# Two triangular inverses moved from 64x64 to 32x32 tiles, in a two-block kernel on one core

## Chip, cores and metric

The kernel runs on one core of a Trainium2 chip, in float32 throughout. The metric is the device time of one execution in microseconds (us); the time before is the median of three runs.

## What is computed

Two blocks of a language model, sequence 512, width 1024. Block one projects its normed input and feeds two mixers, RWKV-7 (8 heads of 64) and stick-breaking attention (8 heads of 64). Block two is a gated delta rule run in both directions (16 value heads of 128, 8 key heads), then a mixture of 32 experts and an embedding gate. What matters here are two linear recurrences:

```python
# RWKV-7, per head
sa = einsum(state, -kk_t)
state = state * w_t + sa * b_t + v_t * k_t
# gated delta rule, chunked
lhs = eye + einsum(k * beta, k) * decay * (1 - eye)
u = triangular_solve(lhs, v * beta)
w = triangular_solve(lhs, k * beta * exp(gc))
```

Both are computed in chunks of 128 steps. A chunk needs T = (I - N)^-1 for a strictly triangular 128x128 matrix N (the sign is folded into N).

## The kernel before

**The inverse by doubling.** T starts as the identity. Level lv (0 to 6, `LEVELS = 7`) joins diagonal blocks of 2^lv rows into blocks of twice the size: the new off-diagonal part is T N T, restricted to that part. Level 0 copies N's own entries. Each level 1 to 6 computes V = N T^T in one set of matmuls, brings V and T to SBUF as operands, computes T V in a second set and writes the wanted entries into T^T. Up to level 5 all that is not zero lies in two 64x64 blocks on the diagonal, so the kernel keeps these alone, 64 columns side by side, and works in 64x64 tiles of TensorE, one on rows 0 to 63 and one on rows 64 to 127. Level 6 (`top`) joins the two halves off the diagonal. `quad[:, lv]` is the byte mask of the entries that a level adds; `copy_predicated` writes them.

**First loop** (L550 to L732 on TensorE, body run four times, once for each pair of RWKV heads; three in a hardware loop, the last apart). TensorE's order is: stick-breaking scores and remainders, the decay and gate products, Q and A (L621, L626), the levels (L648 to L675), the scan over four chunks (L690 to L719), then the norm's sums (L722, L726). For each of two heads h a level issues V (L659, L656 at the top) and, by a product with the identity, T turned round (`flipped`, L638); ScalarE copies both to SBUF (L825, L828); then TensorE issues T V (L674) and VectorE writes the masked part into `TTc` (L1021, after `hold`, a copy of one column at L185). Between levels stand the stick-breaking outputs (L645) and one sum of squares (L668). POOL copies the two finished diagonal blocks into `TT_` (L915) after level 5. `NEXT` lists six products of 8 matmuls that the next pair needs (L539, 128x512 each). `fill` puts 40 of these 48 matmuls into the scan, ten to a chunk by `SLOT = [0, 3, 5, 8, 10]`, behind RU (L694, L695), U (L704), S1 (L710, L711) and Y (L716 to L718); eight more stand between the sums. The stick-breaking weights for them are waited for in chunk 0. In the last pair nothing fills the scan. L572 (the stick-breaking gate product, bank 7) waits for both instructions of L952.

**Heads** (Python loop, unrolled: a first head, seven turns, a last part). A turn projects and convolves q, k, v of one key head while the scan of the head before runs between the products (L1315, L1337 to L1374); then come two z parts (L1326), and `levels` (L1422 to L1478). A head has 16 matrices (four chunks, two directions, two value heads), in two groups g of eight. N^T is formed by a product with the identity (L1430). A level runs V g0, V g1, T g0, T g1 (V: L1449, T: L1471), so that one group's copies lie beside the other's products. ScalarE copies V (L1673); VectorE writes the masked entries into `TTgc` (L1966) and turns them with `transpose`, which works on 32x32 blocks inside a row of partitions (L1971). The top level is L1445 and L1457, the last products L1471, and VectorE scales the result by beta into `TTg` (L2008, L1992). Behind level 2 stand the tokens of v (L1403), behind level 3 those of k (L1410), in level 5 the turned outputs (L1419), behind level 5 the z part 2, at the top the z part 3 (16 matmuls of the trace each, L1326). VectorE also does the attention masks (L1955), silu, and the norm of the outputs (L1930, L1935, L1949) between the levels.

Each engine runs its instructions in the order in which they are written; a `Steps` counter and a semaphore link them (`.at("V 0 3")` is the point at which V of group 0, level 3 was done). `admitted` only counts.

## Time and profile before

| | us |
|---|---|
| median of three runs | 2036.21 |
| lowest, highest | 2033.58, 2037.46 |
| the profiled execution's own time | 2028.58 |
| its span | 2026.8 |
| setup, to the first products | 81.7 |
| one pair of the first loop (first three) | 127 to 129 |
| one turn of the heads | 91.0 |

Times in the profile count from the start of the span. PE is TensorE's matmuls, PEld its weight loads, DVE VectorE, ACT ScalarE, POOL GpSimd. One float32 matmul of the code is two matmuls (and two weight loads) in the profile.

### The profile page before, as it was taken

How to read it: one execution, taken by the hardware profiler on the slowest of the kernel's cores; microseconds unless marked ns; L12 is line 12 of the kernel's file. 1: busy time of each engine (PE TensorE's matmuls, PEld its weight loads, DVE VectorE, ACT ScalarE, POOL GpSimd, SP SyncE). 2: the span in 40 equal slices, each digit the busy share in tenths (PEclk: the TensorE clock that was granted, in tenths of full speed). 3: DMA queues.
4: the chain of work that ended last, by engine and by line, in shares of the span. 5: the costliest groups of instructions: out<-in, count | busy, mean ns of one | idle time of the engine just before them, and what ended most of it. 6: DMA issues, size and time to landing. Idle time of an engine off the chain costs nothing.

```text
span 2026.8 us, 38852 instructions
## 1 busy us (share of the span) xinstructions
PE 1742.4 (86%) x16211; PEld 1135.6 (56%) x16211; DVE 907.8 (45%) x1907; ACT 631.6 (31%) x1208; POOL 127.7 (6%) x247
## 2 busy tenths in 40 slices
PE   0799999999988889999999999999699647777777
PEld 0447466574663457768686777768544523333333
DVE  5223061340621355868677686868402531111162
ACT  1133152431520153545445363545200101111112
POOL 8201000010000000000000000000000010000020
PEclk9999999999977999999999999999899669999989
DMA  8211030110821221111112111111040069999851
GB/s 321 65 43 45 0 86 2 42 45 0 305 90 52 70 66 43 43 43 44 44 42 84 44 43 43 43 43 44 15 166 11 32 253 413 407 417 397 360 176 42
DMA packets 122364, 229.15 MB, mean 113 GB/s; under 512 B 9294, under 2 KB 92587, under 8 KB 109931
## 3 DMA queue, kind: packets, MB, share of 16 engines
q1 hardware_dynamic: 100480, 194.40, 26.6%
q10 hardware_dynamic: 17996, 24.24, 3.3%
q0 software_dynamic: 3744, 8.40, 1.2%
q8 instruction: 114, 1.87, 0.4%
q14 instruction: 30, 0.25, 0.0%
HBM read 203.81 MB, written 28.44 MB: 115 GB/s over the span
## 4 chain that ended last, share of the span: by engine, by line
PE 45%; DVE 11%; DMA 10%; issue 1%; ACT 1%; SPq 0%; DVEq 0%; POOL 0%; ACTq 0%; POOLq 0%
PE ps L1315 11%; DMA W<-in_moe_w_up_dram 9%; PE ps L2209 6%; PE ps L1326 4%; PE ps L2517 4%; PE ps L1085 3%; PE ps L1471 3%; PE ps L2675 2%; PE ps L1449 2%; DVE W L1966 2%; PE ps L1354 1%; PE ps L1364 1%; PE ps L1374 1%; DVE W L1971 1%; DVE arena L1849 1%
## 5 line engine op out<-in xcount | busy, mean ns | idle before, releaser
L1315 PE MATMUL ps<-hT,W 128*128 128x512 f32 x512 | 230.2, 594 | 1.4 <-ACT hT L1109 1.0
L2517 PE MATMUL ps<-W,yT 128*32 128x256 f32 x2048 | 125.4, 400 | 45.4 <-DMA W<-in_moe_w_up_dram 33.9
L1315 PEld LDWEIGHTS ps<-hT,W 128*128 128x128 f32 x512 | 94.9, 190 | 98.2 <-issue 96.4
L539 PE MATMUL ps<-hT,W 128*128 128x512 f32 x288 | 137.9, 612 | 0.0
L2517 PEld LDWEIGHTS ps<-W,yT 128*32 128x32 f32 x2048 | 69.3, 115 | 106.7 <-DMA W<-in_moe_w_up_dram 41.1
L1326 PE MATMUL ps<-W,hT 128*128 128x256 f32 x512 | 117.3, 382 | 0.0
L2209 PE MATMUL ps<-W,yT 128*128 128x512 f32 x256 | 112.2, 601 | 0.9 <-ACT yT L1662 0.9
L1326 PEld LDWEIGHTS ps<-W,hT 128*128 128x128 f32 x512 | 94.8, 190 | 12.7
L1449 PE MATMUL ps<-W,arena 64*64 64x64 f32 x2560 | 89.9, 222 | 13.9 <-DVE W L1966 13.3
L1849 DVE SCALAR_TENSOR_TENSOR arena<-ps,arena 128x510 f32<-128x510 f32 (+1 forms) x128 | 95.6, 747 | 13.8 <-ACT arena L1584 10.4
L1449 PEld LDWEIGHTS ps<-W,arena 64*64 64x64 f32 x2560 | 82.6, 137 | 21.4 <-issue 20.2
L1471 PE MATMUL ps<-W 64*64 64x64 f32 x2816 | 94.0, 220 | 0.1
L1673 ACT ACTIVATE W<-ps 128x512 f32<-128x512 f32 x96 | 57.3, 597 | 110.3 <-PE ps L1449 64.9
L1471 PEld LDWEIGHTS ps<-W 64*64 64x64 f32 x2816 | 88.5, 135 | 4.2 <-issue 4.0
L2209 PEld LDWEIGHTS ps<-W,yT 128*128 128x128 f32 x256 | 49.3, 193 | 63.3 <-issue 63.3
L2533 PE MATMUL ps<-W,arena 128*32 128x512 f32 x512 | 59.9, 610 | 22.9 <-ACT arena L2568 14.3
L539 PEld LDWEIGHTS ps<-hT,W 128*128 128x128 f32 x288 | 51.5, 192 | 49.7 <-issue 48.9
L1966 DVE COPY_PREDICATED W<-quad,ps 128x512 f32<-128x512 uint8 x96 | 69.0, 718 | 0.0
L185 DVE COPY spare<-ones 128x1 f32<-128x1 f32 x152 | 21.5, 142 | 95.5 <-PE ps L674 63.8
L2599 DVE COPY yT<-ps 128x512 f32<-128x512 f32 x32 | 20.6, 686 | 96.9 <-PE ps L2533 96.9
L2546 ACT ACTIVATE arena<-arena 128x256 f32<-128x256 f32 x48 | 20.0, 416 | 139.6 <-DVE arena L2590 138.6
L1085 PE MATMUL ps<-W,yT 128*128 128x512 f32 x128 | 58.1, 617 | 5.4 <-DVE yT L1055 5.4
(474 smaller groups left out, 2938.7 us busy)
## 6 DMA issues: line engine op xcount, KB each, us to landing
W<-in_moe_w_gate_dram SPq DMA_DIRECT2D x32, 1024.0 KB, 10.4
W<-in_moe_w_up_dram SPq DMA_DIRECT2D x32, 1024.0 KB, 10.7
W<-in_moe_w_down_dram SPq DMA_DIRECT2D x32, 1024.0 KB, 10.8
W<-in_w_in_dram SPq DMA_DIRECT2D x33, 512.0 KB, 6.9
W<-in_gdn_w_in_dram SPq DMA_DIRECT2D x16, 1024.0 KB, 6.9
expert_rows<-zeros ACTq DMA_DIRECT2D x1, 15360.0 KB, 56.5
W<-in_gdn_w_in_dram SPq DMA_DIRECT2D x16, 512.0 KB, 4.9
arena<-gate_rows SPq DMA_DIRECT2D x16, 512.0 KB, 6.0
```

What stands on the lines that cost most here:

```text
L539: mm = pe.matmul(ps[:, 5 + i % 2, :], w[:, k, j, :], hT[:, k, :], start=(k == 0), stop=(k == ND - 1))
L1085: mm = pe.matmul(ps[:, 2 * t + h, :], yT[:, k, t * P:(t + 1) * P], wo1(k)[:, 512 * h:512 * h + 512], start=(k == 0), stop=(k == ND - 1))
L1315: mm = pe.matmul(ps[:, 6 + k0 % 2, :], wg[:, k, j * P:(j + 1) * P], hT[:, k, :], start=(k == 0), stop=(k == ND - 1))
L1326: mm = pe.matmul(ps[:, 4 if t < 2 else 1, 256 * (t % 2):256 * (t % 2) + 256], hT[:, k, t * P:(t + 1) * P], wz[:, k, :], start=(k == 0), st ...
L1449: mm = pe.matmul(small(3 * g, m)[q, :], Nn[q, 2 * g + m // 4, m % 4, q], TTgc[q, g, m, :], start=True, stop=True)
L1471: mm = pe.matmul(small(3 * g + 2, m)[q, :], Tgc[q, g, m, :], Vgc[q, g, m, :], start=True, stop=True)
L1673: act.activation(Vgc[:, g, :, :].rearrange("p m t -> p (m t)"), ps[:, 3 * g, :], ACT.Copy).then_inc(*s.act.step(f"V {g} {lv}"))
L1849: link(dve.scalar_tensor_tensor(out=cv[:, j, to], in0=raw[:, of], scalar=taps[:, w, j:j + 1], in1=cv[:, j, to], op0=ALU.mult, op1=ALU.add) ...
L1966: dve.copy_predicated(TTgc[:, g, :, :].rearrange("p (c b) t -> p c b t", c=2), masked(lv), tiles4(ps[:, 3 * g + 2, :]))\
L2209: mm = pe.matmul(ps[:, 2 * t + h, :], yT[:, 4 * c + k, t * P:(t + 1) * P], ring[c % 3][:, k, 512 * h:512 * h + 512], start=(c == 0 and k = ...
L2517: mm = pe.matmul(ps[c0:c0 + m, 2 + j, 0:HID], xgT[:, b, k, c0:c0 + m], weights(j, lane)[:, k, :], start=(k == 0), stop=(k == ND - 1))
L2533: mm = pe.matmul(ps[c0:c0 + m, 5 + h, :], hgT[:, b, f, c0:c0 + m], weights(2, lane)[:, f, 512 * h:512 * h + 512], start=(f == 0), stop=(f ...
```

## The change

- Both inverses: levels 1 to 4 are computed on four 32x32 blocks per 128 rows (`QUARTER`), in four tiles of 32 rows by 32 columns on the diagonal of the array; level 5 (`joined`) joins pairs of them off the diagonal, in 32x32 tiles; level 6 is as it was. What is copied, masked and turned in levels 0 to 5 is 32 columns wide instead of 64.
- After level 4 VectorE multiplies the narrow T^T by a block pattern (`of128`, `of64`) into the full one, zeros included (`onto_diagonal`), and level 5 copies its joins into that (`join`, and two copies per head in the first loop). POOL's copies and the memset of zeros are gone.
- First loop: T of levels 1 to 5 is turned on VectorE (`turned`), no longer by TensorE and ScalarE; the top's flip goes to bank 7 for the second head. Eight of the 48 next products (the stick-breaking q) stand in the levels: two before level 1, one each behind levels 3 and 4, two behind 5, one in the top and one after it. The scan gets eight a chunk (`SLOT = [0, 2, 4, 6, 8]`). The wait for the stick-breaking weights moves ahead of level 1. The step `sig clamped` is split, and L572 waits for the first half alone.
- Heads: z part 2 is split behind levels 1 and 3, z part 3 behind level 4 and at the top. ScalarE's identity loses three waits, and its target is another part of `W`.
- Setup: `quad` has five levels of 32 columns and `identc` 32; POOL writes them in quarters (80 casts instead of 48), without a wait after each.

```diff
-        for lv in range(LEVELS - 1):
+        for lv in range(LEVELS - 2):
...
-            for e in range(2):
-                er = slice(e * HD, e * HD + HD)
+            for r in range(4):
+                er = slice(r * QB, r * QB + QB)
                 for s, q in ((0, q1), (1, q1), (2, q0), (3, q0)):
-                    link(pool.tensor_copy(quad[er, lv, s, :], q[er, er]))
+                    pool.tensor_copy(quad[er, lv, s, :], q[er, er]).then_inc(*su_pool.step())
+            pool.wait_ge(*su_pool.last())
...
-    TTc = take(2, NT, HD)
     Vc = take(2, NT, HD)
+    Ts, Vs = [ap[:, 1, :, :].rearrange("p c t -> p (c t)").rearrange("p (h c t) -> p h c t", h=2, c=NT) for ap in (Tc, Vc)]
     HALF = (slice(0, HD), slice(HD, P))
+    QUARTER = [slice(r * QB, r * QB + QB) for r in range(4)]
...
-        SLOT = [0, 3, 5, 8, 10]
+        SLOT = [0, 2, 4, 6, 8]
...
-            pe.wait_ge(*rw_dve.at("sig clamped", n))
+            pe.wait_ge(*rw_dve.at("sig clamped 0", n))
...
+
+                q = HALF[0]
                 for c in range(NT):
-                    for q in halves:
-                        mm = pe.matmul(ps[q, 2 + 3 * h, c * HD:(c + 1) * HD], TTc[q, h, c, :], ident[q, q], start=True, stop=True)
+                    mm = pe.matmul(ps[q, (2, 7)[h], c * HD:(c + 1) * HD], TT_[q, h, c, q], ident[q, q], start=True, stop=True)
                 mm.then_inc(*rw_pe.step(name))
+
+            def among_levels(lo, hi):
+
+                if not last:
+                    next_products(n, lo, hi)
+                elif hi == ND:
+                    rw_pe.skip(NEXT[0][2])
...
+            if not last:
+                pe.wait_ge(*sb_in.at("in", n))
+            among_levels(0, 2)
             for lv in range(1, LEVELS):
-                top = lv == LEVELS - 1
+                top, joined = lv == LEVELS - 1, lv == LEVELS - 2
                 for h in range(2):
                     pe.wait_ge(*rw_dve.at(f"T {h} {lv - 1}", n))
                     pe.nop().then_inc(admitted, 1)
                     for c in range(NT):
                         if top:
-                            mm = pe.matmul(ps[HALF[0], 1 + 3 * h, c * HD:(c + 1) * HD], N_[HALF[1], h, c, HALF[0]], TTc[HALF[1], h, c, :], start=True, stop=True)
+                            mm = pe.matmul(ps[HALF[0], 1 + 3 * h, c * HD:(c + 1) * HD], N_[HALF[1], h, c, HALF[0]], TT_[HALF[1], h, c, HALF[1]], start=True, stop=True)
+                        elif joined:
+                            for e in range(2):
+                                to, of = QUARTER[2 * e:2 * e + 2]
+                                mm = pe.matmul(ps[to, 1 + 3 * h, c * QB:(c + 1) * QB], N_[of, h, c, to], TTs[of, h, c, :], start=True, stop=True)
                         else:
-                            for q in HALF:
-                                mm = pe.matmul(ps[q, 1 + 3 * h, c * HD:(c + 1) * HD], N_[q, h, c, q], TTc[q, h, c, :], start=True, stop=True)
+                            for r in QUARTER:
+                                mm = pe.matmul(ps[r, 1 + 3 * h, c * QB:(c + 1) * QB], N_[r, h, c, r], TTs[r, h, c, :], start=True, stop=True)
                     mm.then_inc(*rw_pe.step(f"V {h} {lv}"))
-                    flipped(h, f"T {h} {lv}", HALF[0:1] if top else HALF)
+                    if top:
+                        flipped(h, f"T {h} {lv}")
...
+                if top:
+                    among_levels(6, 7)
                 for h in range(2):
-                    pe.wait_ge(*rw_act.at(f"T {h} {lv}", n))
+                    pe.wait_ge(*rw_act.at(f"T {h} {lv}" if top else f"V {h} {lv}", n))
+                    if not top:
+                        pe.wait_ge(*rw_dve.at(f"turned {h} {lv}", n))
                     pe.nop().then_inc(admitted, 1)
                     for c in range(NT):
-                        for q in HALF[0:1] if top else HALF:
+                        if top:
+                            q = HALF[0]
                             mm = pe.matmul(ps[q, 3 + 3 * h, c * HD:(c + 1) * HD], Tc[q, h, c, :], Vc[q, h, c, :], start=True, stop=True)
+                        else:
+                            for r in QUARTER[::2] if joined else QUARTER:
+                                mm = pe.matmul(ps[r, 3 + 3 * h, c * QB:(c + 1) * QB], Ts[r, h, c, :], Vs[r, h, c, :], start=True, stop=True)
                     mm.then_inc(*rw_pe.step(f"TT {h} {lv}"))
+                if lv in (3, 4, 5):
+                    among_levels(lv - 1 if lv < 5 else 4, lv if lv < 5 else 6)
+            among_levels(7, ND)
             for h in range(2):
                 pe.wait_ge(*rw_dve.at(f"T {h} {LEVELS - 1}", n))
-                pe.wait_ge(*rw_pool.at(f"TT {h}", n))
...
-                    next_products(n, 10 * c + SLOT[slot], 10 * c + SLOT[slot + 1])
+                    next_products(n, ND + 8 * c + SLOT[slot], ND + 8 * c + SLOT[slot + 1])
...
+                    if lv < LEVELS - 1:
+                        act.activation(Vs[:, h, :, :].rearrange("p c t -> p (c t)"), ps[:, 1 + 3 * h, 0:NT * QB], ACT.Copy)\
+                           .then_inc(*rw_act.step(f"V {h} {lv}"))
...
                 hold(dve).then_inc(*rw_dve.step())
-                for q in HALF:
-                    dve.copy_predicated(TTc[q, h, :, :], repeat(quad[q, 0, 0, :], NT), Q[q, h, :, 0, q]).then_inc(*rw_dve.step(f"T {h} 0"))
+                for r in QUARTER:
+                    dve.copy_predicated(TTs[r, h, :, :], repeat(quad[r, 0, 0, :], NT), Q[r, h, :, 0, r]).then_inc(*rw_dve.step(f"T {h} 0"))
+
+            def turned(lv):
+
+                for h in range(2):
+                    dve.wait_ge(*rw_dve.at(f"T {h} {lv - 1}", n))
+                    dve.transpose(Ts[:, h, :, :].rearrange("p c t -> p (c t)"), TTs[:, h, :, :].rearrange("p c t -> p (c t)"))\
+                       .then_inc(*rw_dve.step(f"turned {h} {lv}"))
+
+            def onto_diagonal(h):
+
+                dve.tensor_tensor(TT_[:, h, :, :].rearrange("p c (r t) -> p c r t", r=4), TTs[:, h, :, :].unsqueeze(2).to_broadcast([P, NT, 4, QB]),
+                                  of128[:].unsqueeze(1).unsqueeze(3).to_broadcast([P, NT, 4, QB]), ALU.mult).then_inc(*rw_dve.step(f"diagonal {h}"))
+
+            turned(1)
...
+                    if lv < LEVELS - 2:
+                        hold(dve).then_inc(*rw_dve.step())
+                        dve.copy_predicated(TTs[:, h, :, :], repeat(quad[:, lv, 0, :], NT), ps[:, 3 + 3 * h, 0:NT * QB].rearrange("p (c t) -> p c t", c=NT))\
                            .then_inc(*rw_dve.step(f"T {h} {lv}"))
+                    elif lv < LEVELS - 1:
+                        dve.wait_ge(*rw_dve.at(f"diagonal {h}", n))
+                        for e in range(2):
+                            to, of = QUARTER[2 * e:2 * e + 2]
+                            dve.tensor_copy(TT_[to, h, :, of], ps[to, 3 + 3 * h, 0:NT * QB].rearrange("p (c t) -> p c t", c=NT))\
+                               .then_inc(*rw_dve.step(f"T {h} {lv}"))
                     else:
                         dve.tensor_copy(TT_[HALF[0], h, :, HALF[1]], ps[HALF[0], 3 + 3 * h, 0:NT * HD].rearrange("p (c t) -> p c t", c=NT))\
                            .then_inc(*rw_dve.step(f"T {h} {lv}"))
+                if lv < LEVELS - 2:
+                    turned(lv + 1)
+                if lv == LEVELS - 3:
+                    for h in range(2):
+                        onto_diagonal(h)
...
+        def z_part(s, t, ks=range(ND)):
+
...
-            for k in range(ND):
+            for k in ks:
...
+                    for r in QUARTER:
+                        mm = pe.matmul(tiny(3 * g + 2, m)[r, :], Nn[r, 2 * g + m // 4, m % 4, r], ident[r, r], start=True, stop=True)
...
+                        elif joined:
+                            for m in (0, 2, 1, 3, 4, 6, 5, 7):
+                                for to, of in across(m):
+                                    mm = pe.matmul(tiny(3 * g, m)[to, :], Nn[of, 2 * g + m // 4, m % 4, to], TTgs[of, g, m, :], start=True, stop=True)
                         else:
                             for m in range(8):
-                                for q in HALF:
-                                    mm = pe.matmul(small(3 * g, m)[q, :], Nn[q, 2 * g + m // 4, m % 4, q], TTgc[q, g, m, :], start=True, stop=True)
+                                for r in QUARTER:
+                                    mm = pe.matmul(tiny(3 * g, m)[r, :], Nn[r, 2 * g + m // 4, m % 4, r], TTgs[r, g, m, :], start=True, stop=True)
...
+                        z_part(s, 3, range(4, ND))
...
+                            if top:
+                                q = HALF[m % 4 // 2]
                                 mm = pe.matmul(small(3 * g + 2, m)[q, :], Tgc[q, g, m, :], Vgc[q, g, m, :], start=True, stop=True)
+                            else:
+                                for r in [to for to, of in across(m)] if joined else QUARTER:
+                                    mm = pe.matmul(tiny(3 * g + 2, m)[r, :], Tgs[r, g, m, :], Vgs[r, g, m, :], start=True, stop=True)
                         mm.then_inc(*s.pe.step(f"T {g} {lv}"))
+                if lv == 1:
+                    z_part(s, 2, range(4))
                 if lv == 2:
                     v_tokens(s)
                 if lv == 3:
                     k_tokens(s)
-                if lv == 5:
-                    z_part(s, 2)
+                    z_part(s, 2, range(4, ND))
+                if lv == 4:
+                    z_part(s, 3, range(4))
 
...
+            act.activation(TTgs.rearrange("p g m t -> p (g m) t"), repeat(identc[:], 16), ACT.Copy).then_inc(*s.act.step("identity"))
...
+                    if lv < LEVELS - 1:
+                        act.activation(Vgs[:, g, :, :].rearrange("p m t -> p (m t)"), ps[:, 3 * g, 0:8 * QB], ACT.Copy).then_inc(*s.act.step(f"V {g} {lv}"))
...
         def put_blocks(s, g, lv):
             hold(dve).then_inc(*s.dve.step())
-            dve.copy_predicated(TTgc[:, g, :, :].rearrange("p (c b) t -> p c b t", c=2), masked(lv), tiles4(ps[:, 3 * g + 2, :]))\
+            dve.copy_predicated(TTgs[:, g, :, :].rearrange("p (c b) t -> p c b t", c=2), masked(lv), tiles4(ps[:, 3 * g + 2, 0:8 * QB]))\
...
+            dve.wait_ge(*s.dve.at(f"T {g} {lv}", s.i))
+            dve.transpose(Tgs[:, g, :, :].rearrange("p m t -> p (m t)"), TTgs[:, g, :, :].rearrange("p m t -> p (m t)"))\
+               .then_inc(*s.dve.step(f"turned {g} {lv + 1}"))
+
+        def onto_diagonal(s, g):
+
+            dve.tensor_tensor(TTgc[:, g, :, :].rearrange("p m (r t) -> p m r t", r=2), TTgs[:, g, :, :].unsqueeze(2).to_broadcast([P, 8, 2, QB]),
+                              of64[:].unsqueeze(1).unsqueeze(3).to_broadcast([P, 8, 2, QB]), ALU.mult).then_inc(*s.dve.step(f"diagonal {g}"))
+
+        def join(s, g, lv):
+
+            dve.wait_ge(*s.dve.at(f"diagonal {g}", s.i))
+            for d in range(2):
+                for to, of in across(2 * d):
+                    cols = slice(of.start % HD, of.start % HD + QB)
+                    dve.tensor_copy(tiles4(TTgc[:, g, :, :].rearrange("p m t -> p (m t)"))[to, :, 2 * d:2 * d + 2, cols],
+                                    tiles4(ps[:, 3 * g + 2, 0:8 * QB])[to, :, 2 * d:2 * d + 2, :]).then_inc(*s.dve.step(f"T {g} {lv}"))
...
-                        put_blocks(s, g, lv)
+                        (put_blocks if lv < LEVELS - 2 else join)(s, g, lv)
...
+                if lv == LEVELS - 3:
+                    for g in range(2):
+                        onto_diagonal(s, g)
```

## Rows read from the trace of the kernel before

**Rows 1.** Page, part 1: TensorE, busy us, share of the span, instructions.

```profile
PE 1742.4 (86%) x16211; PEld 1135.6 (56%) x16211; DVE 907.8 (45%) x1907; ACT 631.6 (31%) x1208; POOL 127.7 (6%) x247
```

**Rows 2.** Busy time of each engine by stretch; columns as the first line says.

```profile
core 0: us, PE busy (x) PEld busy (x) DVE busy (x) ACT busy (x) POOL busy (x), PEclk, DMA share, GB/s
...
300.10:324.10 24.00, 22.24 (x547) 18.94 (x547) 8.69 (x31) 11.03 (x28) 2.88 (x4) 1.00 0.01 3
324.10:377.00 52.90, 52.90 (x209) 26.86 (x210) 3.23 (x8) 5.09 (x13) 1.26 (x1) 1.00 0.00 1
...
582.10:627.90 45.80, 33.55 (x132) 22.01 (x133) 7.23 (x14) 4.70 (x12) 1.26 (x1) 0.50 0.00 1
...
1117.50:1154.90 37.40, 35.27 (x854) 32.29 (x853) 27.39 (x57) 16.08 (x28) 0.00 (x0) 1.00 0.01 3
```

**Rows 3.** TensorE in order of time, Q's end, then a head's levels: start us, us [idle before].

```profile
297.51 0.39 PE L626 MATMUL ps<-arena 64*128 64x128 f32 x4
...
1117.50 2.08 PE L1430 MATMUL ps<-ident,arena 64*64 64x64 f32 x64
1120.14 1.15 PE L1449 MATMUL ps<-W,arena 64*64 64x64 f32 x32 [0.56 <-DVE W L1966]
...
1124.62 1.15 PE L1449 MATMUL ps<-W,arena 64*64 64x64 f32 x32
...
1130.06 2.08 PE L1449 MATMUL ps<-W,arena 64*64 64x64 f32 x64
...
1138.77 1.15 PE L1449 MATMUL ps<-W,arena 64*64 64x64 f32 x32
...
1154.85 3.70 PE L1315 MATMUL ps<-hT,W 128*128 128x512 f32 x8
```

**Rows 4.** Pace: three TensorE rows in order of time, then the top level's start.

```profile
277.94 7.31 PE L592 MATMUL ps<-W,hT 128*128 128x128 f32 x64
...
1098.56 3.60 PE L1315 MATMUL ps<-hT,W 128*128 128x512 f32 x8
...
1148.63 0.51 PE L1445 MATMUL ps<-W,arena 64*64 64x64 f32 x10
1148.92 0.27 PE L1457 MATMUL ps<-ident,W 64*64 64x64 f32 x2
1148.97 0.28 PE L1445 MATMUL ps<-W,arena 64*64 64x64 f32 x3
...
1148.62:1150.12 1.50, 1.50 (x65) 1.43 (x64) 0.00 (x0) 0.76 (x2) 0.00 (x0) 1.00 0.00 0
```

**Rows 5.** Groups of instructions: forms, count, busy us, mean ns of one, idle before.

```profile
L1673 ACT ACTIVATE W<-ps 128x512 f32<-128x512 f32 x96 | 57.3, 597 | 110.3 <-PE ps L1449 64.9 <-PE ps L1445 45.0
L825 ACT ACTIVATE arena<-ps 128x256 f32<-128x256 f32 x40 | 15.3, 383 | 43.4 <-PE ps L659 42.0
L1966 DVE COPY_PREDICATED W<-quad,ps 128x512 f32<-128x512 uint8 x96 | 69.0, 718 | 0.0
L1021 DVE COPY_PREDICATED arena<-quad,ps 128x256 f32<-128x256 uint8 x40 | 17.3, 432 | 0.0
L1971 DVE STREAM_TRANSPOSE W<-W 128x512 f32<-128x512 f32 x80 | 56.9, 711 | 2.7
L1992 DVE TENSOR_TENSOR W<-ps,arena 64x128 f32<-64x128 f32 x64 | 15.7, 284 | 48.0 <-PE ps L1471 47.2
L572 PE MATMUL ps<-hT,W 128*128 128x512 f32 x64 | 28.5, 599 | 6.2 <-DVE arena L952 6.2
```

**Rows 6.** SyncE's queue, 255 to 330 us: when the stick-breaking weights are issued.

```profile
285.43 4.22 SPq L505 DMA_DIRECT2D W<-in_w_in_dram  x4
```

**Rows 7.** Transfers issued from 285 to 297 us: count, KB, median us to landing.

```profile
W<-in_w_in_dram SPq DMA_DIRECT2D x4, 512.0 KB, 6.1
```

**Rows 8.** POOL in order of time: its first instruction after setup.

```profile
81.69 0.10 POOL L884 MEMSET arena<- 128x3 f32 x1 [24.65 <-ACT hT L258]
```

**Rows 9.** TensorE in order of time, first head, level 1.

```profile
756.96 3.46 PE L1449 MATMUL ps<-W,arena 64*64 64x64 f32 x64 [3.20 <-DVE W L1966]
```

79 lines of the change are left out of this document (37 added, 42 removed).

## The prediction

> **What bounds the kernel now.** I began with the page. TensorE is busy for 86% of the span and is the largest share of the chain that ended last [rows 1]: an edit pays if it shortens TensorE's stream, or a wait that stands in it. The busy time by stretch comes next [rows 2]. One pass of the first loop's levels (300.1 to 324.1) holds 22.24 us of TensorE in 24.00, the scan behind it 52.90 in 52.90, one head's levels 35.27 in 37.40. So TensorE binds all three, VectorE is second in a head's levels (27.39 us), and work taken out of the levels is time until a wait appears. The last pair's scan is the exception: 33.55 us in 45.80, at a granted clock of 0.50 (1.2 GHz).
>
> Third, the order of time on TensorE in one head [rows 3]. A group (V or T of one g) is 16 matmuls of the code and 32 in the trace; 64 of them take 2.08 us, of which 0.22 is the last one's tail: 29 ns each, 0.94 us a group. Levels 1, 2, 3, 5 and 6 begin 2.6, 7.1, 12.6, 21.3 and 31.1 us after N^T (1117.50), and the next head 37.4 us after it.
>
> **The pace of a 32x32 tile.** A matmul costs one tile 429 ns at 512 columns (8 in 3.60 us) and 112 ns at 128 (64 in 7.31 us) [rows 4]. At 64 columns two tiles share a 29 ns pace, so each has 58 ns. Each halving of the columns halves the cost, but for some 5 ns. At 32 columns that gives 27 + 5 = 32 ns; the bounds are 29 (half of 58) and 58 (nothing falls). The four diagonal tiles differ in rows and columns. At the sixth level four 64x64 tiles do run at once: 64 of the 65 matmuls there start between 1148.62 and 1150.12 less the 0.22 tail, 20 ns each, although each code line uses only two tiles, and L1457 starts at 1148.92 while L1445 is unfinished [rows 4]. So the program's order does not hold a free tile back. A group of 64 matmuls is then 64 / 4 x 32 = 0.51 us instead of 0.94. Level 5 keeps 32 matmuls: 0.26 us. In the first loop V and T fall from 16 matmuls at 29 ns (0.47 us) to 32 at 8 ns (0.26 us), and the flip by TensorE (another 0.47 us per h) is gone in levels 1 to 5.
>
> The Trainium skill, "TensorEngine Tiling (Array Packing)", section "Instruction Overhead", speaks against this: one free column costs as much as 60, and no tiling factor should be taken from a side that is already small. By that rule a tile stays near 58 ns and TensorE wins nothing in the heads. No row here has a 32-wide tile with 32 moving columns; it is the first rival below.
>
> **VectorE and ScalarE.** Copy-predicated is 718 ns at 512 elements and 432 at 256 [rows 5]: 0.43 in the heads, and 0.29 at the first loop's 128 by the same step. The transpose is 711 at 512; halved with the same fixed part 0.44 at 256 and 0.28 at 128 (bounds 0.36 and 0.71). ScalarE's V copy goes from 597 to 383 ns at 256 columns, about 0.28 at 128. Added per head: two placements on the diagonal at 0.68 (512 elements, like L1966 less its mask), and eight joining copies at 0.26 (nearest L1992, 284 ns alone, overlapping a little) for the two L1966 of level 5. VectorE falls from 27.4 to about 23.6 us a head.
>
> **One head, walked.** I laid the instructions in the program's order on three queues with these durations, 0.04 us from an engine's end to a waiting one and 0.15 to TensorE's next matmul (as between such pairs throughout the trace). The chain of a level is then V 0.51 + tail 0.19 + 0.04 + copy 0.38 + 0.15, T 0.51 + 0.19 + 0.04 + hold and copy 0.50 + 0.15 = 2.66 us, so a level cannot be shorter; its TensorE work is 4 x 0.51 = 2.05 plus the filler. Walked with the durations of before, levels 2, 3, 5, 6 and the end come at 7.2, 12.5, 21.4, 31.1 and 36.9 us against the measured 7.1, 12.6, 21.3, 31.1 and 37.4. With the new ones they come at 7.8, 11.1, 20.1, 25.4 and 29.7. Levels 1, 3 and 4 carry half a z part each (eight matmuls at 256 columns, half of 429 ns: 1.73 us), which fills the wait for VectorE; without that move the walk gains 2 us less. Gain **7.2 us a head**, 7.9 in the first head (no scan work on VectorE). The transpose's upper bound takes 0.8 back. Behind the levels the next head's four first products (3.4 us) still cover VectorE's last scaling, as now. Heads: 7 x 7.2 + 7.9 = **58 us**.
>
> **The first loop.** The same walk (before: 25.6 us from the last products of Q and A to the scan, measured 324.1 - 297.9 = 26.2) [rows 2, 3] gives 20.7: 4.9 us less, though eight products (8 x 0.858 = 6.9 us) now stand in it. They come out of the scan, where TensorE is busy throughout; each chunk keeps two products behind RU, U, S1 and Y, 1.72 us at each, more than what they cover (a tail of 0.22, a copy under L825's 0.38, 0.19 for the two hand-overs). So the scan gives 6.9 us in full: 11.8 us a pair, three pairs, 35 us. The last pair has no products: its levels give 6.9 us (flips and half tiles), its scan nothing. The products need the stick-breaking weights, now awaited before level 1, with all of the levels queued behind that wait on TensorE: the transfers are issued from 285.4 over 4.2 us and land 6.1 us after issue [rows 6, 7], by 296, ahead of 297.5, the last products of Q and A. No transfer and nothing on SyncE's queue is moved. The split of the clamp's step lets L572 start one 0.7 us instruction earlier; TensorE waits 6.2 us there in four passes [rows 5]: 2.8 us. VectorE's new work, four first copies per h instead of two (+0.2 us), ten turns (2.8), two placements (1.4), lies beside fillers and is in the walk. POOL's copies into T^T (L915) ended before level 6 did: 0. First loop: 35 + 7 + 3 = **45 us**.
>
> **Setup.** 80 casts instead of 48 (L306) and ten memsets, less one level of masks. At 0.56 us each the casts add 18 us; POOL waits 24.65 us behind them [rows 8], so 0. If they took 1 us each, some 10 us would show.
>
> **The clock.** It stood at 1.2 GHz where TensorE had waited: over the last scan, and at level 1 of the first head, after 3.20 us idle, where two groups took 3.46 us instead of 1.9 [rows 2, 9]. The shorter levels wait more: about 22 us of work in 29.7. I allow one such dip (1.6 us) in under half of the twelve stages and a longer one in the last pair, whose levels have no filler: **8 us** lost.
>
> **Sum.** 58 + 45 - 8 = 95 us. The profiled execution took 2028.6 us (span 2026.8); that gives 1933.6. The median of the runs is 2036.2, 7.6 above it, and I carry that over: **1941 us**.
>
> **Rivals.**
> 1. The small matmul does not get cheaper: 58 ns a tile at 32 columns. A head's group stays 0.94 us; the walk gives 2.9 us a head (first 2.1) from VectorE, ScalarE and the moved z parts: 22 us. First loop: 9.2 a pair, 4.8 in the last, 2.8 for the clamp: 35 us. Result 1979. For it: nothing here has 32 columns, and it is the skill's rule. Against: halving has held from 512 to 64. 15%.
> 2. Tiles do not run four at a time in this order: each tile's two successive matmuls hold the queue, so two start per 32 ns, 16 ns each. Group 1.02 us: 1.7 us a head, 8.6 a pair, 7 for the last pair and the clamp, 45 in all. Result 1991. Against it: the early start at 1148.92. 6%.
> 3. Slower: the number of matmuls is what costs. TensorE takes one start per 29 ns whatever the tile, because its instructions come no faster, and a level has twice as many. Group 1.87 us; the walk loses 16.6 us a head, 134 in all, the first loop gains 8: 2162. It turns at about 20 ns per matmul, where heads lose 31 us and the first loop gains 26. For it: today's steady pace is 29 ns in every group. Against: the 20 ns at the sixth level, where only tile occupancy should bind. 8%. The Trainium skill, "TensorE: Matmul & The Clock Gate", Part 1, states a floor of about 25 ns from start to start; by that the sum would be some 70 us slower. The 20 ns stretch speaks against a floor common to all tiles.
> 4. The clock falls in most stages: two more dips in each of twelve, 40 us: 1981. Against: in 1117.5 to 1154.9 it held 1.00, though the array is half empty. 6%.
> 5. The change leaves the time as it is (a miscount on my side, or all gains met by new waits): 2%.
>
> **Numbers.** The forecast has 63%, with its own range 1920 to 1960 (the pace between 26 and 35 ns, no dips or twice as many). To hold 8 in 10 the range reaches to rivals 1 and 4: 1918 to 1984. A measurement tells 0.2%, some 4 us. Faster: 63 + 15 + 6 + 6 = 90, less a little: 0.89. Same 0.02. Slower 0.09.
>
> **What would show it.** Right: L1449's and L1471's successors take about 0.7 us per 64 matmuls (0.51 and a tail), a head's levels about 30 us, copy-predicated 0.43, turns 0.44, the first loop's levels about 21 us and its scan 46. Wrong: groups of 0.94 us or more (rivals 1 to 3; with four starts close together and then a pause it is rival 1, evenly spaced it is 2 or 3); a granted clock under 0.95 in the heads (rival 4); or idle TensorE before V put down to VectorE for more than 1 us a level, which would mean that the new copies cost more than I took.

## The result, and the profile after

The changed kernel takes **2084.51 us** (median of four runs, 2073.19 to 2091.87) against 2034.89 for the kernel before, measured beside it (median of four): a ratio of 1.0241, 95% interval 1.0191 to 1.0291. The forecast was 1941, faster, with a range of 1918 to 1984. It was wrong in sign, and the time lies 144 us above it. The profiled execution took 2085.35 us.

The page of the changed kernel, parts 1 and 3; the first line answers to [rows 1]; q8 is the instruction queue (transfers, MB, share):

```profile
PE 1720.4 (83%) x21203; PEld 1078.8 (52%) x21203; DVE 892.4 (43%) x2011; ACT 590.6 (28%) x1168; POOL 113.3 (5%) x268
...
q8 instruction: 154, 2.52, 0.5%
```

TensorE executes 4992 more matmuls than before and as many more weight loads, and is busy 22 us less; yet the span is 56.8 us longer (2083.6). So it stands still more. What ended those waits is in the chain of waits, TensorE from 742 to 1440 us, seven heads (columns: waited for, us in total, times, longest):

```profile
PE ps L1550 <- issue: 53.1, 33, 2.7
PE ps L1524 <- issue: 9.0, 9, 1.6
PE ps L1524 <- DVE W L2048: 7.9, 7, 2.0
```

L1550 is the successor of L1471 (T), L1524 that of L1449 (V). "Issue" means that the profile shows nothing that TensorE waited for. In the kernel before the same stretch has no issue idle worth a row. In the first loop (130 to 640 us) L685, V, stands 15.5 us for the same reason.

One head in order of time (start us, us, idle before; L1397 is z, L1501 is N^T), to be set beside [rows 3]:

```profile
1145.06 1.35 PE L1501 MATMUL ps<-ident,arena 32*32 32x32 f32 x128
1147.43 0.63 PE L1524 MATMUL ps<-W,arena 32*32 32x32 f32 x50 [1.02 <-DVE W L2048]
1149.03 0.91 PE L1524 MATMUL ps<-W,arena 32*32 32x32 f32 x78 [0.97 <-issue]
1149.93 0.61 PE L1550 MATMUL ps<-W 32*32 32x32 f32 x49
1152.93 1.29 PE L1550 MATMUL ps<-W 32*32 32x32 f32 x79 [2.39 <-issue]
1154.14 3.78 PE L1397 MATMUL ps<-W,hT 128*128 128x256 f32 x8
...
1159.25 0.53 PE L1550 MATMUL ps<-W 32*32 32x32 f32 x39
1161.49 1.40 PE L1550 MATMUL ps<-W 32*32 32x32 f32 x89 [1.71 <-issue]
...
1166.33 0.44 PE L1550 MATMUL ps<-W 32*32 32x32 f32 x29
1168.89 1.59 PE L1550 MATMUL ps<-W 32*32 32x32 f32 x99 [2.12 <-issue]
...
1176.29 1.42 PE L1550 MATMUL ps<-W 32*32 32x32 f32 x128
```

Two things stand in these lines. While it runs, the small matmul is as cheap as forecast: 128 in 1.35 us, less a tail of 0.22, are 8.9 ns each, 0.57 us per 64 (forecast 0.51; before 0.94 for 32). And TensorE breaks off in the middle of a group, after 49, 39 or 29 matmuls, for 1.7 to 2.4 us, where the program has no wait. Counted through all of the head's lines, 127, 254, 254, 381 and 126 matmuls lie from one stop to the next: the stops stand at multiples of about 127 matmuls, that is 254 TensorE instructions with the weight loads, and not every multiple has one.

Busy time by stretch, the changed kernel, answering to [rows 2]: a head's levels, the stretch between two heads' levels, one first-loop pair from Q's end to the scan, its scan:

```profile
core 0: us, PE busy (x) PEld busy (x) DVE busy (x) ACT busy (x) POOL busy (x), PEclk, DMA share, GB/s
1145.00:1189.40 44.40, 33.99 (x1429) 28.45 (x1428) 23.89 (x63) 13.75 (x28) 0.00 (x0) 0.81 0.02 4
1189.40:1243.10 53.70, 53.38 (x224) 34.83 (x219) 39.69 (x95) 27.90 (x59) 0.00 (x0) 1.00 0.25 79
293.70:326.50 32.80, 27.38 (x659) 15.30 (x659) 13.59 (x50) 7.21 (x20) 0.00 (x0) 0.84 0.01 2
326.50:372.50 46.00, 46.00 (x194) 23.79 (x194) 3.23 (x8) 4.77 (x13) 0.72 (x1) 1.00 0.00 1
```

A head's levels take 44.4 us instead of 37.4; what follows them is as before. The first head's N^T starts at 751.18 (before 751.68), the last head's at 1440.13 (before 1390.31): seven turns of 98.42 us against 91.23. So the heads lost 7.2 us each, 57 in all, and all that stands ahead of the first head gained 0.5 us.

### The profile page after: what moved, and what is told of

Read it like the earlier page. It is cut to its first block, busy times and chain, and to the rows that moved or that the text cites. A ratio compares the mean times of both kernels' runs of the same rounds, so it can differ in the third digit from the quotient of the medians.

```text
span 2083.6 us, 48936 instructions
## 1 busy us (share of the span) xinstructions
PE 1720.4 (83%) x21203; PEld 1078.8 (52%) x21203; DVE 892.4 (43%) x2011; ACT 590.6 (28%) x1168; POOL 113.3 (5%) x268
## 3 DMA queue, kind: packets, MB, share of 16 engines
q8 instruction: 154, 2.52, 0.5%
## 4 chain that ended last, share of the span: by engine, by line
PE 46%; DMA 9%; DVE 8%; issue 5%; ACT 1%; SPq 0%; DVEq 0%; POOL 0%; ACTq 0%; POOLq 0%
PE ps L1386 11%; DMA W<-in_moe_w_up_dram 9%; PE ps L2306 5%; PE ps L1397 4%; PE ps L2614 4%; PE ps L1550 3%; PE ps L1145 3%; PE ps L1524 2%; PE ps L2772 2%; PE ps L1425 1%; DVE arena L1931 1%; PE ps L1445 1%; PE ps L1435 1%; PE ps L1408 1%; PE ps L1412 1%
## 5 line engine op out<-in xcount | busy, mean ns | idle before, releaser
L1386 PE MATMUL ps<-hT,W 128*128 128x512 f32 x512 | 230.9, 595 | 1.5 <-ACT hT L1169 1.1
L2614 PE MATMUL ps<-W,yT 128*32 128x256 f32 x2048 | 130.3, 412 | 41.4 <-DMA W<-in_moe_w_up_dram 28.7
L551 PE MATMUL ps<-hT,W 128*128 128x512 f32 x288 | 148.5, 640 | 4.2 <-DVE spare L189 4.2
L1397 PE MATMUL ps<-W,hT 128*128 128x256 f32 x512 | 145.0, 439 | 1.5 <-issue 1.5
L1397 PEld LDWEIGHTS ps<-W,hT 128*128 128x128 f32 x512 | 110.1, 224 | 19.9 <-issue 1.9
L1550 PE MATMUL ps<-W 32*32 32x32 f32 x4608 | 65.9, 211 | 61.0 <-issue 60.5
L2306 PE MATMUL ps<-W,yT 128*128 128x512 f32 x256 | 112.3, 601 | 0.9 <-ACT yT L1741 0.9
L1550 PEld LDWEIGHTS ps<-W 32*32 32x32 f32 x4608 | 57.6, 123 | 68.3 <-issue 66.5
L1753 ACT ACTIVATE W<-ps 128x256 f32<-128x256 f32 x80 | 29.9, 383 | 135.8 <-PE ps L1524 97.8
L1524 PE MATMUL ps<-W,arena 32*32 32x32 f32 x4096 | 49.2, 200 | 20.5 <-issue 11.3
L1145 PE MATMUL ps<-W,yT 128*128 128x512 f32 x128 | 57.4, 611 | 5.5 <-DVE yT L1115 5.5
L2772 PE MATMUL ps<-W,yT 128*128 128x512 f32 x128 | 58.1, 612 | 3.8 <-ACT yT L2794 3.8
L1524 PEld LDWEIGHTS ps<-W,arena 32*32 32x32 f32 x4096 | 44.0, 112 | 32.6 <-issue 32.5
## 6 DMA issues: line engine op xcount, KB each, us to landing
W<-in_moe_w_gate_dram SPq DMA_DIRECT2D x32, 1024.0 KB, 10.5
```

The source lines that it names most:

```text
L551: mm = pe.matmul(ps[:, 5 + i % 2, :], w[:, k, j, :], hT[:, k, :], start=(k == 0), stop=(k == ND - 1))
L1145: mm = pe.matmul(ps[:, 2 * t + h, :], yT[:, k, t * P:(t + 1) * P], wo1(k)[:, 512 * h:512 * h + 512], start=(k == 0), stop=(k == ND - 1))
L1386: mm = pe.matmul(ps[:, 6 + k0 % 2, :], wg[:, k, j * P:(j + 1) * P], hT[:, k, :], start=(k == 0), stop=(k == ND - 1))
L1397: mm = pe.matmul(ps[:, 4 if t < 2 else 1, 256 * (t % 2):256 * (t % 2) + 256], hT[:, k, t * P:(t + 1) * P], wz[:, k, :], start=(k == 0), st ...
L1524: mm = pe.matmul(tiny(3 * g, m)[r, :], Nn[r, 2 * g + m // 4, m % 4, r], TTgs[r, g, m, :], start=True, stop=True)
L1550: mm = pe.matmul(tiny(3 * g + 2, m)[r, :], Tgs[r, g, m, :], Vgs[r, g, m, :], start=True, stop=True)
```

## Experiments

**Instructions in a long burst (rate).** The burst stands ahead of the first head's N^T in the kernel before, three times, as `burst(512, rows, wide)`: rows 32 and 32 columns, rows 64 and 32 columns, rows 64 and 64 columns:

```
+            for i in range(count // len(pieces)):
+                for r in pieces:
+                    c = wide * (i % 4)
+                    pe.matmul(ps[r, 2, c:c + wide], Nn[r, 0, 0, r], ident[r, r.start:r.start + wide], start=True, stop=True)
...
```

> The kernel before, with three bursts of 512 matmuls of the code (1024 records each) ahead of the first head's N^T, on its operands and into its bank, whose results are overwritten: in 32x32 tiles at 32 columns, in 64x64 tiles at 32 columns, in 64x64 tiles at 64 columns, each followed by eight matmuls at 512 columns. Theory A (TensorE's instructions are fetched in pieces of 256, and in a long burst they come no faster than some 3 us a piece): the first burst runs at 8 to 9 ns a record for its first 150 to 250 records and then stops for 1 to 2.5 us once or twice per 256 records, 20 to 24 ns a record on average, 20 to 25 us in all; the second has the same average, although its tiles are larger; the third stays at 29 ns a record, 30 us, without a stop. Rival B (the stops in the changed kernel come from something in the levels, such as the waits or the fallen clock, not from the number of instructions): the first burst takes 1024 x 8.8 ns = 9 us without a stop.

TensorE in order of time, first burst:

```profile
756.39 2.19 PE L1427 MATMUL ps<-ident,arena 32*32 32x32 f32 x236
760.69 1.90 PE L1427 MATMUL ps<-ident,arena 32*32 32x32 f32 x128 [2.11 <-issue]
764.14 1.93 PE L1427 MATMUL ps<-ident,arena 32*32 32x32 f32 x128 [1.55 <-issue]
767.87 1.93 PE L1427 MATMUL ps<-ident,arena 32*32 32x32 f32 x128 [1.79 <-issue]
```

Busy time by stretch, one row for each of the three bursts:

```profile
756.30:782.30 26.00, 14.17 (x1025) 13.17 (x1024) 2.72 (x5) 3.43 (x5) 0.00 (x0) 0.59 0.02 4
792.20:822.30 30.10, 30.10 (x1026) 29.98 (x1025) 0.00 (x0) 0.00 (x0) 0.00 (x0) 1.00 0.02 4
829.30:859.40 30.10, 30.10 (x1026) 30.00 (x1025) 0.00 (x0) 0.00 (x0) 0.00 (x0) 1.00 0.02 4
```

236 matmuls at 8.4 ns, then exactly 128 (256 instructions) per 3.45 to 3.73 us. That is theory A's pattern; B's 9 us is out. The average beyond the first 236 is 27 to 29 ns, above A's 20 to 24, and the whole burst took 26 us where A had 20 to 25. What A had wrong besides is the second burst: 64x64 tiles at 32 columns cost (30.10 - 0.22) / 1023 = 29.2 ns a matmul, the same as at 64 columns, without a stop.

**The same at full clock (rate2).** In the first burst the clock stood at 0.59 in the mean. Here `burst(32 or 64 matmuls, 32, 32)` alternates with `wide(1)` or `wide(2)`, matmuls of 512 columns.

> The kernel before, with three patterns ahead of the first head's N^T, set apart by eight matmuls at 512 columns: 16 times (64 records of 32x32 matmuls and two 512-column matmuls of the code), 16 times (64 records and one 512-column matmul), 8 times (128 records and one 512-column matmul). The wide matmuls keep the granted clock at 1.00. Theory A (a piece of 256 instructions takes some 3 us from one request to the next at full clock): the first has no stops (about 4.3 us of work per 256 instructions), 36 us in all; the second (2.65 us of work per 256) has stops that bring 256 instructions to about 3.1 us; the third (1.9 us of work per 256) has stops of some 1.2 us each. Rival B (stops come with the fallen clock alone): no stops in any of the three, 36, 23 and 16 us.

The third pattern in order of time, one cycle:

```profile
853.64 1.13 PE L1431 MATMUL ps<-arena 128*128 128x512 f32 x2
854.70 0.95 PE L1427 MATMUL ps<-ident,arena 32*32 32x32 f32 x88
856.91 0.55 PE L1427 MATMUL ps<-ident,arena 32*32 32x32 f32 x40 [1.26 <-issue]
857.39 1.12 PE L1431 MATMUL ps<-arena 128*128 128x512 f32 x2
```

Busy time by stretch, one row for each of the three patterns:

```profile
763.00:806.00 43.00, 43.00 (x1092) 21.69 (x1091) 0.00 (x0) 0.00 (x0) 0.00 (x0) 1.00 0.01 3
812.00:841.00 29.00, 27.95 (x1056) 15.32 (x1056) 0.00 (x0) 0.00 (x0) 0.00 (x0) 1.00 0.02 4
848.70:876.00 27.30, 18.82 (x1040) 12.33 (x1039) 0.00 (x0) 0.00 (x0) 0.00 (x0) 1.00 0.02 4
```

The clock is 1.00 throughout and the stops are there: 3.75 us per cycle of 260 instructions in the third pattern, 14.4 ns an instruction. In the first, 136 instructions per 2.60 us, none; in the second, 132 per 1.74 us (13.2 ns each), two short ones (0.55 us in the eighth cycle, 0.33 in the tenth). So TensorE is supplied with one instruction per 14.4 ns, **29 ns a matmul with its weight load**, at either clock (3.45 to 3.73 us per 256 are 13.5 to 14.6 ns in the first burst), and some 470 instructions (236 matmuls) can stand ready. More did not gather, although the products ahead of the first burst are slow and few. The sizes in the expectation were off (a hand-over adds 0.3 us to each wide group, and a piece takes 3.7 us, not 3), the verdict is not.

**Half the matmuls left out (half).** Two of the four tiles are left out of the heads' V and T at levels 1 to 4:

```
-                                for r in QUARTER:
+                                for r in QUARTER[::2]:
...
-                                for r in [to for to, of in across(m)] if joined else QUARTER:
+                                for r in [to for to, of in across(m)] if joined else QUARTER[::2]:
```

> The changed kernel, with half of the matmuls of the heads' V and T groups at levels 1 to 4 left out (two of the four 32-row tiles; the values of those blocks are then not the inverse's). Theory A (instruction supply): a level of a head has one fetch of 256 instructions instead of two, the idle time of TensorE before the T and V groups put down to issue falls from 62 us to under 15, and a head's turn from 98.5 us to 84 to 90; the whole below 2010 us. Rival B (the granted clock falls by itself because the array is emptier, and that is the loss): with half the work the clock in the heads stays at 0.92 or falls further, and the heads keep most of their loss; the whole stays above 2040 us.

Result 1988.55 us, one run. Of the 62.1 us of issue idle before V and T in seven heads, 4.2 are left in eight (TensorE's waits, 742 to 1440 us):

```profile
PE ps L1524 <- DVE W L2048: 10.4, 16, 2.0
PE ps L1524 <- issue: 4.2, 7, 0.7
```

A turn is 86.8 us ((1349.65 - 742.00) / 7) instead of 98.4. Its work is half, so this is no price of the change; it shows that the number of instructions makes the stops. The instruction queue says the same: 122 transfers instead of 154, for 4096 matmuls and as many weight loads fewer, which is 256 instructions a transfer. It does not clear the clock: from 742 to 1350 us the granted clock is 0.96 (before: 1.00), and the one head with a mean of 0.74 in its first 33 us took 90.7 us where the one ahead of it took 85.9 (0.95 in its levels). Both have 0.7 us of issue idle, so the 4.8 us between them are not stops.

**The filler spread (spread).**

```
+                    elif st == 1 and lv < 5:
+                        z_part(s, *((2, range(0, 2)), (2, range(4, 6)), (2, range(6, 8)), (3, range(0, 2)))[lv - 1])
...
-                    z_part(s, 2, range(4))
+                    z_part(s, 2, range(2, 4))
...
```

> The changed kernel, with the z part's matmuls placed in pairs between V and T and behind T of levels 1 to 4 instead of in fours behind a level; the same work and the same number of instructions. Theory A (instruction supply): each pair (0.86 us) covers part of a fetch that now stands open, idle put down to issue in the heads falls from 62 to about 35 to 45 us, the heads gain 3 to 5 us each, and the whole comes to 2045 to 2065 us. Rival B (clock by itself): the clock stays at 0.92 in the heads and the time within 10 us of 2084.

2073.97 us (2067.82 to 2082.15), ratio 1.0211 (1.0175 to 1.0247): A's 2045 to 2065 is missed, and the time is at the very edge of B's 10 us. The interval overlaps that of the changed kernel (1.0191 to 1.0291), so no gain is shown; the granted clock from 750 to 1440 us is 0.93 (changed kernel 0.92). The waits from 742 to 1440 us:

```profile
PE ps L1524 <- issue: 32.5, 25, 1.8
PE ps L1552 <- issue: 25.8, 26, 1.7
```

With 4.4 before the join (L1520) that is 62.7 us of issue idle against 64.8 (2.7 before it there): more and shorter stops, nearly the same sum. This run does not support A; that B's cause alone makes stops is ruled out by rate2, where they stand at a clock of 1.00. Why the sum stayed is open. A head's levels execute 1429 matmuls, 2858 instructions, which is 41.2 us at 14.4 ns, close to the measured 44.4. But some 470 of them can stand ready when the levels begin, behind 53.7 us with 224 matmuls; the other 2390 need 34 us. So the supply did not run all the time: what can stand ready is limited, and a filler of 3.6 us behind a full store earns nothing for the groups after it. That a better order exists is neither shown nor excluded.

**The first loop with 64x64 tiles (first64).** The kernel before with the flips on VectorE, the eight products in the levels and the split clamp:

```
+                    dve.transpose(Tc[:, h, :, :].rearrange("p c t -> p (c t)"), TTc[:, h, :, :].rearrange("p c t -> p (c t)"))\
...
-                    flipped(h, f"T {h} {lv}", HALF[0:1] if top else HALF)
+                    if top:
+                        flipped(h, f"T {h} {lv}")
```

> The kernel before, with the first loop's changes except the tiles: the flips of levels 1 to 5 on VectorE, the eight products moved into the levels, the clamp's step split; the tiles stay 64x64, the heads stay as before. Theory A (the number of instructions is what failed in the changed kernel, and the moved products and the flips were right): no idle time put down to issue in the first loop's levels, levels of 25 to 27 us, a scan of 46, a pair some 5 to 6 us shorter than before, the whole 2010 to 2020 us. Rival C (the moved products cannot be covered in the levels, whatever the tiles): levels of 31 us, a pair as long as before, the whole 2025 to 2035 us.

**2005.93 us** (2001.59 to 2010.79), ratio 0.9890 (0.9862 to 0.9917): theory A, slightly better than its 2010 to 2020 in the whole, though the levels took slightly more than its 25 to 27 us. Busy time of first64 from Q's end to the scan, pair 2:

```profile
core 0: us, PE busy (x) PEld busy (x) DVE busy (x) ACT busy (x) POOL busy (x), PEclk, DMA share, GB/s
289.60:317.40 27.80, 25.58 (x405) 16.80 (x405) 13.97 (x46) 8.28 (x20) 2.88 (x4) 1.00 0.01 2
```

27.8 us at a clock of 1.00, against 32.8 at 0.84 with the small tiles (its row in the section on the result). The first head's N^T starts at 728.54, 22.6 us earlier than in the changed kernel. So the small tiles with what goes with them (the narrow copies, the placement, the casts in the setup) cost 22.6 us ahead of the heads, and the rest of the first loop's change was worth 23.1.

**Stop or empty array (firsthalf2).** Half of the first loop's V and TT at levels 2 to 4 left out, level 1 whole (with level 1 halved too there is no measurement):

```
-                            for r in QUARTER:
+                            for r in QUARTER[::1 if lv == 1 else 2]:
...
-                            for r in QUARTER[::2] if joined else QUARTER:
+                            for r in QUARTER[::1 if lv == 1 else 2]:
```

> The changed kernel, with half of the matmuls of the first loop's V and TT groups at levels 2 to 4 left out (two of the four tiles; the values of those blocks are then not the inverse's); level 1 is whole. The heads stay as in the changed kernel. In the changed kernel the first loop's levels (293.7 to 326.5 us) hold 3.1 us of idle time put down to issue, and the clock is at 1.2 GHz from 308.2 to 318.4. Theory A (the stops for instructions come first and the clock falls after them): with fewer instructions at most one stop at level 1, the clock stays at 1.00 through levels 2 to 6 of the first three pairs, and the stretch from the last products of Q and A to the scan falls from 32.8 to 23 to 25 us. Rival D (the clock falls because 32x32 tiles leave the array nearly empty, whether or not TensorE stops): no stops at levels 2 to 4 either, but the clock falls in most pairs, and the stretch stays at 27 to 31 us.

Busy time in levels 1 to 3, then in the rest of the levels, pair 2:

```profile
core 0: us, PE busy (x) PEld busy (x) DVE busy (x) ACT busy (x) POOL busy (x), PEclk, DMA share, GB/s
296.00:301.60 5.60, 5.08 (x170) 3.88 (x169) 3.67 (x19) 2.09 (x6) 0.00 (x0) 1.00 0.01 3
301.60:315.20 13.60, 13.44 (x148) 6.81 (x148) 4.34 (x15) 1.11 (x4) 0.00 (x0) 0.50 0.01 1
```

**Rival D holds** (2068.56 us, one run), and my theory that the clock falls only behind stops is out: no stop from 289 to 319 us, TensorE busy for 5.08 of 5.60 us in 32x32 tiles (the narrow attention products among them), and then the clock is at 1.2 GHz for 13.6 us. The stretch took 30.0 us (289.5 to 319.5), inside D's 27 to 31. Pair 3 has the same mean clock, 0.77 over 30.1 us. One reading in the expectation is off: in the changed kernel the clock was still 1.00 to 311.0 us and 0.50 from 312.0 to 321.6, not from 308.2 to 318.4. The array was emptier here than in the changed kernel (two tiles of four), so this shows that small tiles are enough to bring the clock down, not how much of it they bring there, where stops come on top.

**Better fillers, and narrow tiles where they add no matmul.** On top of first64: the z part as two matmuls behind each of levels 1, 3, 4 and 5 (first64z); level 5 alone in 32x32 tiles, joined as in the change (first64join); both; and both with the first loop's level 5 back in 64x64 tiles (headsjoin).

```
+                    z_part(s, 2, range(2, 4))
...
+                                for to, of in across(m):
+                                    mm = pe.matmul(tiny(3 * g, m)[to, :], Nn[of, 2 * g + m // 4, m % 4, to], TTgc[of, g, m, within(of)], start=True, stop=True)
```

> The kernel called first64, with the heads' z part spread: two matmuls of it behind each of levels 1, 3, 4 and 5 instead of eight behind level 5; the other eight stay at the sixth level; tiles and work as before. TensorE waits 11.7 us for VectorE before V in eight heads in first64, some 1.5 us a head, and each pair of z matmuls (0.86 us) covers such a wait. Theory A (with 64x64 tiles supply is not the bound, so a filler put into a wait pays): 0.5 to 1 us a head, 4 to 8 us in all below first64, 1998 to 2002 us. Rival (the wait only moves behind level 5, where the eight stood): 2006 us within 3.

> The kernel called first64, with level 5 alone joined in 32x32 tiles at 32 columns, in the heads and in the first loop, out of the 64-wide storage; the number of matmuls is the same as before (16 of the code in a group of a head, 8 in the first loop), V's copy is half as wide, and two or four joining copies take the place of one predicated copy. Theory A (a narrow tile costs as little as forecast, 8.5 to 9 ns a matmul; only the doubled number broke the supply): level 5's four groups in a head fall from 3.8 us to 1.2 to 2.5 us (one piece of 256 instructions falls into them, so up to 1.5 us of a stop), a head gains 0.5 to 2 us, the whole 1992 to 2003 us. Rival (narrow groups lose whatever their number, through stops, the clock or VectorE's four copies): 2006 us or more.

> Both of the edits of first64z and first64join together. Theory A: their gains nearly add, 1988 to 2000 us. Rival: level 5 in narrow tiles, with only two z matmuls behind it, leaves TensorE waiting for VectorE's joining copies, and the sum is no better than the better one of the two.

> The kernel called first64both with the first loop's level 5 back in 64x64 tiles (as in first64); the heads keep the spread z part and level 5 joined in 32x32 tiles. In the traces, the first head's N^T starts at 732.0 us in first64join and first64both and at 728.5 in first64 and first64z, so the first loop's narrow join costs 3.5 us, and without it the whole is 1987 to 1991 us. Rival: that difference lies within what one trace differs from another, and the whole stays at 1993 within 2.

| | median us | ratio to before, 95% | us a head |
|---|---|---|---|
| first64 | 2005.93 | 0.9890 (0.9862 to 0.9917) | 90.9 |
| first64z | 1997.91 | 0.9837 (0.9809 to 0.9866) | 89.7 |
| first64join | 2003.15 | 0.9850 (0.9823 to 0.9877) | 90.4 |
| first64both | 1993.00 | 0.9804 (0.9775 to 0.9833) | 89.2 |
| headsjoin | 1991.72 | 0.9807 (0.9783 to 0.9832) | 89.1 |

Each row was measured beside the kernel before; first64 ran on another chip than the next three and headsjoin on a third, so the ratios compare better than the medians. first64both and headsjoin are 2.0% and 1.9% faster than the kernel before. first64both came out as expected (1988 to 2000); first64z is at the lower edge of its 1998 to 2002, first64join at the upper edge of its 1992 to 2003. Level 5 in small tiles (headsjoin, one head) runs at its cheap pace, since its number of matmuls is that of before:

```profile
1101.11 2.08 PE L1496 MATMUL ps<-W,arena 64*64 64x64 f32 x64
1103.05 2.08 PE L1522 MATMUL ps<-W 64*64 64x64 f32 x64
...
1106.12 0.92 PE L1492 MATMUL ps<-W,arena 32*32 32x32 f32 x64
1108.35 1.09 PE L1462 MATMUL ps<-ident,arena 128*128 128x128 f32 x8 [1.31 <-DVE arena L2008]
1109.37 0.75 PE L1519 MATMUL ps<-W 32*32 32x32 f32 x64
```

0.92 and 0.75 us for 64 instead of 2.08, without a stop; 1.31 of it is handed to a wait for VectorE's gate (L2008, 1.18 us long; in first64z that wait is some 0.1 us a head beyond the first), so a head gains only about 0.5 us (89.7 to 89.2). Against first64, join's interval overlaps, and so does first64both's with first64z's: the small tiles at level 5 are worth 3 to 5 us by the medians and 7 to 8 by the ratios, but neither is clear of the intervals. headsjoin is a miss: its expectation was 1987 to 1991 us from the 3.5 us that the traces showed for the first loop's narrow join, and its rival, 1993 within 2, holds. The first head's N^T does start at 726.49 against 731.97 in first64both, but the profiled run of headsjoin is its fastest of six, 6.2 us under its median.

## Why the prediction was wrong

- **The pace of a 32x32 tile: right.** Forecast 32 ns a tile, 8 ns a matmul; measured 8.9 in the heads. With two of the four tiles at work (half, granted clock 1.00) 64 matmuls take 1.20 us; with the tail of some 0.2 taken off that is 16 ns each, 32 ns a tile:

```profile
1010.58 1.20 PE L1524 MATMUL ps<-W,arena 32*32 32x32 f32 x64
```

  Rival 1 is out for these tiles, though it holds for 64x64 ones: 32 moving columns cost them 29.2 ns, as 64 do. The Trainium skill, "TensorEngine Tiling (Array Packing)", section "Instruction Overhead", sets one free column equal to 60; the second burst agrees (58.4 ns a tile at 32 columns and at 64), the first (four tiles at 8.4 ns, some 34 each) does not. Rival 2 is out as well.
- **The step that failed: "The pace of a 32x32 tile" priced a group by its tiles and took the 20 ns at the sixth level as proof that the supply of instructions is no limit.** That stretch has 65 matmuls, fewer than the 236 that stand ready. In the long run TensorE gets a matmul per 27 to 29 ns (rate, rate2), and the levels' groups stood 62 us for it in seven heads. That was rival 3, held at 8% and priced at 2162: its mechanism is the right one. Its price was too high because it charged every group 29 ns a matmul, while the supply also runs on during fillers and waits: a head's levels took 44.4 us, a loss of 7.0, not 16.6. The 29 ns "steady pace in every group" of before was the warning: 64x64 tiles need as much as the supply gives, so before had no reserve for twice the matmuls. The Trainium skill, "TensorE: Matmul & The Clock Gate", Part 1, has a floor of about 25 ns from start to start; the 8.9 ns here speak against such a floor, and only the long-run 29 ns lie near it.
- **VectorE and ScalarE: right.** The changed kernel's groups, answering to [rows 5]:

```profile
L2051 DVE STREAM_TRANSPOSE W<-W 128x256 f32<-128x256 f32 x80 | 35.6, 445 | 2.8
...
L2048 DVE COPY_PREDICATED W<-quad,ps 128x256 f32<-128x256 uint8 x80 | 34.5, 432 | 0.0
...
L1753 ACT ACTIVATE W<-ps 128x256 f32<-128x256 f32 x80 | 29.9, 383 | 135.8 <-PE ps L1524 97.8 <-PE ps L1520 38.0
...
L2065 DVE COPY W<-ps 32x128 f32<-32x128 f32 x64 | 18.4, 287 | 17.8 <-PE ps L1550 16.2
```

Forecast 0.44, 0.43, 0.38 and 0.26 us; the placement (L2056) takes 0.67 against 0.68.
- **One head: 44.4 us against a walk of 29.7.** The walk had no term for the supply of instructions: the head shown has 8.5 us of issue idle (7.0 before T, 1.0 before V, 0.5 before the join). By turns it is 14.4 us a head (7.2 lost, 7.2 forecast as gained), 115 in all: of the miss of 144, by far the largest part.
- **The first loop: forecast 45, got 0.5.** The scan gave 6.9 us a pair as forecast (52.9 to 46.0), the clamp's wait fell from 6.2 to 3.6 us (forecast 2.8 less). The levels missed: 32.8 us instead of 20.7. Of the 12.1, 3.1 are stops. A mean clock of 0.84 over 32.8 us is 10.5 us at 1.2 GHz (0.16 x 32.8 x 2), with TensorE busy in nearly all of it: some 4.7 lost. Another 3.4 are the walk's own, because first64, with neither, takes 27.8 us where my sum gives 24.4 of TensorE's work (22.24 - 4.7 + 6.9). The rest, 0.9, stays open; the split in three is worked out, not isolated by a run. So from the end of Q and A in the first pair to that in the last the change gained 7.3 us, not 35. The last pair's levels and scan lost 4.6 us where 6.9 was forecast as gained; one of their stops alone is 4.08:

```profile
563.40 0.48 PE L685 MATMUL ps<-arena 32*32 32x32 f32 x20 [4.08 <-issue]
```

  Another 2.8 us net went behind the loop, where the last 60.8 us ahead of the first head, at a granted clock of 0.96, became 64.3 at 0.89 (687 to 751 us). first64 has 64.2 at 0.89 in that stage too, so the small tiles are not the reason there; which part of the change is stays open.
- **The clock: 8 us forecast, and too little.** [rows 2]'s 1.00 in a half-empty array was taken to hold for an emptier one. It does not (firsthalf2). Rival 4's sign, a clock under 0.95 in the heads, came true: 0.92 from 750 to 1440 us, before 1.00. In the head shown (0.81) two z fillers of eight matmuls took 3.78 and 3.62 us where two others took 1.99, and the tokens of v and k 1.97 and 1.11 where headsjoin has 1.09 and 0.66, 4.7 us more for the same work; in half a slow head cost 4.8. How much of the heads' loss is the clock stays open all the same: TensorE might have stood for its instructions in part of that time, and no run had the heads' supply without the fallen clock.
- **Setup: right.** POOL still waits 26.69 us behind the new casts.
- "What would show it" named groups of 0.94 us or more, evenly spaced, for rival 3. The true sign was another: cheap groups, broken off by an issue wait without a semaphore.

## What to carry to other kernels

Count instructions as well as work: a float32 matmul of the code is four TensorE instructions here, and TensorE got 256 of them per 3.5 to 3.7 us over stretches longer than some 470, which is also the most that stood ready. Narrow tiles ran at their cheap pace where they replace matmuls one for one (level 5), though what they gave the whole is not clear of the noise; where they double the matmuls the kernel got slower. Read a stretch for the supply only if it is longer than what stands ready, and look at whether the present pace already equals it.

## What the runs showed of the hardware

- A piece of 256 TensorE instructions arrives as one 16 KB transfer on the instruction queue: the changed kernel has 154 of them (2.52 MB), half has 122 with 8192 TensorE instructions fewer, and the kernel before has 114. The Trainium skill, "Runtime: NRT & Kernel Launch", section "Instruction fetch mechanics", describes such blocks of 256 and calls the cost of crossing one mostly hidden. In 32x32 tiles the runs disagree: 1.5 to 2.1 us per piece stood open in the first burst of rate, 1.0 to 1.3 us in the third pattern of rate2.
- A 64x64 tile has the same pace at 32 moving columns as at 64 (29.2 ns, two tiles at a time), a 32x32 tile at 32 columns takes 32 ns with two at work (half) and some 34 with four (rate).
- The clock fell to 1.2 GHz behind 5.6 us in which TensorE was busy for 5.08, at full clock, without a stop, in 32x32 tiles; in 64x64 tiles (first64, 289.6 to 317.4) it held 1.00.
